# Decode attention beside a Strassen-like feed-forward: summing one step's values directly ahead of the next step's scores

## The reference, cut to what matters

```python
def _sb_block(q_blk, qpos_blk, k, v, k_pos, sb_bias):
    z = jnp.einsum('bqhd,bkhd->bhqk', q_blk, k) * (HEAD_DIM ** -0.5)
    z = z + sb_bias[None, :, None, None]
    mask = k_pos[None, :] < qpos_blk[:, None]
    log1m = jnp.where(mask, jax.nn.log_sigmoid(-z), 0.0)
    suffix = lax.cumsum(log1m, axis=3, reverse=True)
    between = jnp.concatenate([suffix[..., 1:], jnp.zeros_like(suffix[..., :1])], axis=-1)
    a = jnp.where(mask, jnp.exp(jax.nn.log_sigmoid(z) + between), 0.0)
    return jnp.einsum('bhqk,bkhd->bqhd', a, v)
...
past_k = cache_k[l][page_table].reshape(db, past_len, H_SB, HEAD_DIM)
past_v = cache_v[l][page_table].reshape(db, past_len, H_SB, HEAD_DIM)
```

## Time and profile before

| what | value |
|---|---|
| runs before, three | 3337.8, 3342.49, 3342.72 us; median 3342.49 us |
| profiled execution, first to last instruction | 3338.9 us |
| PE matmuls busy | 3206.4 us, 96% |
| PE weight loads busy | 2425.2 us, 73% |
| DVE, ACT, POOL busy | 51%, 34%, 47% |
| moved by DMA | 536.93 MB, mean 161 GB/s |

### The profile page before, as it was taken

One profiled execution on the slowest core, in us unless ns is written; L12 is line 12 of the kernel. 1 busy time (PEld: TensorE's weight loads), 2 busy tenths in 40 slices (PEclk: granted clock), 3 DMA queues, 4 the chain that ended last, 5 costly groups with the idle time before them and its releaser, 6 DMA issues.

```text
span 3338.9 us, 54535 instructions
## 1 busy us (share of the span) xinstructions
PE 3206.4 (96%) x18534; PEld 2425.2 (73%) x18535; DVE 1706.2 (51%) x2588; ACT 1134.6 (34%) x2457; POOL 1578.2 (47%) x1265
## 2 busy tenths in 40 slices
PE   7999999899899899999999999999999999899999
PEld 5777786566566677777777777777777778787777
DVE  4222222499799454545435544454553444665555
ACT  3333333499799333222103312212331220232220
POOL 2322222277576455544445544435554544565553
PEclk9999999999899899999999999999999999999999
DMA  7223311301100567777886767787677655122222
GB/s 275 95 96 118 103 45 37 110 2 52 53 2 14 200 207 254 252 257 249 276 303 209 242 227 234 248 269 258 226 241 234 234 190 172 63 76 76 76 76 83
DMA packets 235494, 536.93 MB, mean 161 GB/s; under 512 B 27599, under 2 KB 57535, under 8 KB 214217
## 3 DMA queue, kind: packets, MB, share of 16 engines
q1 hardware_dynamic: 200072, 354.12, 32.4%
q10 hardware_dynamic: 35137, 179.22, 15.0%
HBM read 498.70 MB, written 34.55 MB: 160 GB/s over the span
## 4 chain that ended last, share of the span: by engine, by line
PE 57%; DVE 6%; issue 2%; DMA 1%; ACT 1%; DVEq 0%; ACTq 0%
PE ff_pB L1694 49%; PE s_pZ L1290 4%; PE s_pO L1304 3%; DVE ff_conv L1986 1%; DVE s_left L1368 1%; DMA ff_w<-in_w_units 1%; DVE ff_act_in L2002 0%; DVE ff_x L1913 0%; ACT ff_conv L1778 0%; PE s_pZ L1296 0%; DVE ff_conv L1988 0%; DVE ff_rs L1995 0%; DVE s_kpage L1979 0%; DVE s_kpage L1976 0%; DVE s_stop L1372 0%
## 5 line engine op out<-in xcount | busy, mean ns | idle before, releaser
L1694 PE MATMUL ff_pB<-ff_act_in,ff_w 128*128 128x256 f32 (+1 forms) x2496 | 617.2, 392 | 22.7 <-ACT ff_act_in L1773 14.6
L1694 PEld LDWEIGHTS ff_pB<-ff_act_in,ff_w 128*128 128x128 f32 x2496 | 475.8, 194 | 133.7 <-issue 45.7
L2042 POOL TENSOR_TENSOR ff_sums<-ff_w 128x512 f32<-128x512 f32 (+1 forms) x152 | 190.4, 1253 | 697.8 <-PE ff_pB L1694 583.1
L1986 DVE SCALAR_TENSOR_TENSOR ff_conv<-ff_raw,k_vecT,ff_conv 128x512 f32<-128x512 f32 x352 | 381.2, 1083 | 91.9 <-ACT ff_raw L1785 85.7
L1913 DVE SCALAR_TENSOR_TENSOR ff_x<-ff_pB,k_mod,ff_x 128x256 f32<-128x256 f32 (+2 forms) x448 | 214.2, 480 | 385.8 <-PE ff_pB L1694 381.9
L1808 ACT ACTIVATE ff_raw<-ff_pB 128x256 f32<-128x256 f32 (+1 forms) x352 | 136.0, 388 | 765.4 <-PE ff_pB L1694 760.0
L1694 PE MATMUL ff_pB<-ff_diff_up,ff_sums 128*128 128x256 f32 (+1 forms) x1600 | 389.0, 385 | 5.6 <-DVE ff_diff_up L1889 5.6
L1184 POOL TENSOR_TENSOR at_stop<-at_stop,at_left 128x512 f32<-128x512 f32 (+3 forms) x320 | 311.5, 998 | 164.5 <-ACT at_stop L1124 160.3
L1962 DVE TENSOR_TENSOR ff_raw<-ff_raw,ff_pB 128x256 f32<-128x256 f32 (+1 forms) x264 | 111.3, 424 | 474.4 <-PE ff_pB L1694 474.4
L1694 PEld LDWEIGHTS ff_pB<-ff_diff_up,ff_sums 128*128 128x128 f32 x1600 | 301.3, 190 | 70.2 <-issue 17.1
L2054 POOL TENSOR_TENSOR ff_raw<-ff_raw,ff_conv 128x512 f32<-128x512 f32 (+1 forms) x88 | 119.3, 1355 | 301.5 <-ACT ff_raw L1791 124.7
(11 more groups left out here) (248 smaller groups left out, 5026.9 us busy)
## 6 DMA issues: line engine op xcount, KB each, us to landing
ff_w<-in_w_units ACTq DMA_DIRECT2D x136, 1024.0 KB, 6.2
s_kpage<-in_cache_k SPq DMA_DIRECT2D x512, 256.0 KB, 4.0
s_vpage<-in_cache_v SPq DMA_DIRECT2D x512, 256.0 KB, 3.1
in_ada<-in_w_ada SPq DMA_DIRECT2D x16, 1024.0 KB, 5.0
ff_w<-in_w_units ACTq DMA_DIRECT2D x16, 768.0 KB, 4.8
in_w<-in_w_in SPq DMA_DIRECT2D x5, 2048.0 KB, 20.1
in_hT<-in_x_cols SPq DMA_DIRECT2D x8, 1024.0 KB, 6.9
wada<-in_w_ada SPq DMA_DIRECT2D x4, 2048.0 KB, 18.2
```

Of the source, the lines that this page charges most:

```text
L1694: last = pe.matmul(into, left[:, kt * P:(kt + 1) * P], right[:, kt, :], start=kt == 0 and p in (1, 2, 5), stop=kt == depth(j) - 1, skip_gr ...
L1986: ins = dve.scalar_tensor_tensor(cv, raw[:, f % 2, half, i:i + CT], tap, cv, ALU.mult, ALU.add)
L2042: pool.tensor_tensor(S3, A11, A21, ALU.subtract).then_inc(sums_ready, 1)
```

## The change

The list of a chunk used to hold four entries per step (SCORE, WEIGH, MOVE, SUM), each placed by itself, evenly. Now it holds three: the SUM of the step before together with SCORE, then WEIGH, then MOVE. SUM of the very last step is an entry of its own. The entries are still spread evenly over the products. No instruction is added or taken away, and no buffer or semaphore is changed.

```diff
-    pieces = [(q, i) for q in steps for i in (SCORE, WEIGH, MOVE, SUM)]
+    pieces = []
+    for q in steps:
+        pieces += [[(q - 1, SUM)] * (q > 0) + [(q, SCORE)], [(q, WEIGH)], [(q, MOVE)]]
+        if q == NSTEP - 1:
+            pieces.append([(q, SUM)])
...
-            plan.append(("sa",) + pieces[placed])
+            plan += [("sa",) + piece for piece in pieces[placed]]
```

## The result

| kernel | median, lowest to highest | ratio to the kernel before, 95% interval |
|---|---|---|
| before | 3340.14 us, 3335.5 to 3342.72 (4 runs) | |
| changed | 3367.65 us, 3357.09 to 3372.01 (4 runs) | 1.0083 [1.0068, 1.0098] |

The change makes the kernel slower by 0.8%, 27.5 us. The forecast of 3333 us and its range up to 3348 are both missed, and the sign is the other one. The profiled execution has a span of 3370.3 us against 3338.9, at the upper end of the runs.

The account below looks back on a forecast made before the run. The prediction took PE to bound the kernel. Its terms, -20.5 - 4 + 2 + 13 = -9.5 us on a 3338.9 us span, gave 3329.4, plus 3.6 to the runs' median: 3333 us, range 3319 to 3348.

Parts of the forecast that it names:

- The visits: PE at SUM and SCORE: 63 joined visits save 0.33 us each if the seam is free, together 20.5 us.
- case D: Rival, between SUM and SCORE: the seam costs what a visit does, giving 3349 us; chance 0.05.
- The distance from SCORE to MOVE: More room from SCORE and WEIGH to MOVE ends PE's waits for `s_stop`: 4 us gained.
- case E: Rival, on DVE and ACT: WEIGH and copies hold up products elsewhere, +5 us, giving 3338; chance 0.12.
- The norms: WEIGH directly ahead of the reciprocal lengthens PE's `ff_act_in` waits in chunks two and three: +2 us; first chunk even.
- The pages: K pages late for SCORE in twelve steps: 14.4 us, less 1.4 of `ff_x` waits, so +13.
- The walk: Step-by-step count of late K pages, steps 2 to 63, arrival minus step length less earlier lateness: 14.4 us.
- my own bound: Upper bound for late K pages: 28.9 us if each page arrives 1 us later.
- case C: Rival, K pages late by more: the page loop paces the first chunk; 3349 us at 1 us more; chance 0.13.
- the signs that I had named: Refuting readings: `s_kpage` row missing or above 25 us, SUM-to-SCORE starts above 1.9, `ff_x` and `ff_raw` waits up 5.
- The sum: All terms on the span of 3338.9 us: -20.5 - 4 + 2 + 13 = -9.5 us.

## Why the prediction was wrong, point by point

**The visits: right.** The price of a visit was read correctly and the seam is free (1.74 us from SUM to SCORE). Of the 20.5 us, 16 were measured in the kernel that has nothing else, with 20.5 inside its interval. My case D, a seam that costs what a visit does, is out: its sign was starts above 1.9 us apart.

**The distance from SCORE to MOVE: the step that failed.** I counted room between WEIGH and MOVE and took 4 us of gain, as if the old waits for `s_stop` were the only thing that WEIGH's place decides. Two things were wrong with that. The room for MOVE moves most of those waits and does not remove them: DVE is as late as before, and the product that needs the next take of `ff_raw` waits instead of MOVE (5.5 us in 8 cases for 4.0 in 8, with MOVE alone moved). And WEIGH is 1.4 to 3.4 us of DVE in a list that DVE must walk in order; its later place sets it ahead of other work, above all of additions to `ff_x` and of the norm. Measured, the new places cost 16 to 18 us, of which MOVE's place has 0.12%, 4 us and within the intervals of nothing, and WEIGH's the rest. I had this as case E with 5 us and a chance of 0.12, priced as "half as much again" of the old waits for `ff_x`, with no reading of what stands around WEIGH at its new places. This is step 11 in the changed kernel, DVE first, then POOL and PE:

```profile
1434.68 1.53 DVE L1990 SCALAR_TENSOR_TENSOR ff_conv<-ff_raw,k_vecT,ff_conv 128x512 f32<-128x512 f32 x2
1436.12 0.15 DVE L1381 COPY s_left<-s_left 128x1 f32<-128x1 f32 x1
1436.31 1.86 DVE L1368 TENSOR_TENSOR_SCAN s_left<-s_go,s_left 128x256 f32<-128x256 f32 x1
1438.20 1.30 DVE L1372 TENSOR_TENSOR s_stop<-s_stop,s_left 128x256 f32<-128x256 f32 x1
1439.43 0.86 DVE L1917 SCALAR_TENSOR_TENSOR ff_x<-ff_pB,k_mod,ff_x 128x256 f32<-128x256 f32 x2
...
1436.35 1.27 POOL L2058 TENSOR_TENSOR ff_raw<-ff_raw,ff_conv 128x512 f32<-128x512 f32 x1 [5.70 <-DVE ff_conv L1990]
1437.70 1.52 POOL L2060 TENSOR_TENSOR ff_hidden<-ff_raw,ff_conv 128x512 f32<-128x512 f32 x1
...
1439.96 3.56 PE L1698 MATMUL ff_pB<-ff_diff_down,ff_sums 128*128 128x256 f32 x8 [2.26 <-DVE ff_x L1917]
1443.35 1.89 PE L1698 MATMUL ff_pB<-ff_hidden,ff_sums 128*128 128x256 f32 x8
```

And the same step on DVE in the kernel before, where no product waits at this place:

```profile
1428.10 0.75 DVE L1368 TENSOR_TENSOR_SCAN s_left<-s_go,s_left 128x256 f32<-128x256 f32 x1
1428.89 0.42 DVE L1372 TENSOR_TENSOR s_stop<-s_stop,s_left 128x256 f32<-128x256 f32 x1
1429.23 0.48 DVE L1913 SCALAR_TENSOR_TENSOR ff_x<-ff_pB,k_mod,ff_x 128x256 f32<-128x256 f32 x1
1429.62 1.53 DVE L1986 SCALAR_TENSOR_TENSOR ff_conv<-ff_raw,k_vecT,ff_conv 128x512 f32<-128x512 f32 x2
```

At its old place WEIGH stood ahead of the last two taps and was done in 1.3 us. At the new one it stands behind them and directly ahead of the additions to `ff_x`, and takes 3.3 us. PE waits 2.26 us for an addition, and then runs at the lower clock: granted 0.61 on the mean of 1440 to 1444 us, with 3.39 us from this product's start to the next one's and not 1.73.

**The norms: right in the second and third chunk, wrong in the first.** The wait for `ff_act_in` rose from 11.2 to 12.6 us in sum. In the first chunk I set gain against loss at nothing; MOVE's wait there was 3.05 us, with a slower clock behind it.

**The pages: the right mechanism, mis-sized.** Twelve late steps were forecast and twelve came, steps 3 and 55 among them, though not all the same ones: step 21, my worst case, was not late. That the number agrees is in part luck. The walk gave 14.4 us and I took 13; the waits were 21.7. By my own bound a mean lateness of half a microsecond more does that, but I have not found where it comes from: the median landing was 3.9 us, not longer than the 4.2 of before. SP's idle time under SUM, which I had expected to shrink, grew from 426.0 to 457.0 us in 63 waits. What I left out altogether is what comes with such waits: the slower clock behind the long ones, and weights that come late (8.5 us against 1.2; 4.5 when pages are issued fast). The experiments price the late pages with all that at 26 to 28 us, twice my term. So case C, at 0.13, is what happened in size, together with E. Of the signs that I had named, that of E came (waits for `ff_x` and `ff_raw` grew by 11.7 us, with 5 as the border); that of C did not (21.7 us for `s_kpage`, with 25 as the border), because the border left out the clock and the weights.

**The sum.** -16 (visits) + 17 (places) + 27 (pages) = 28 us, and 27.5 were measured; since the terms are differences of the same four kernels, this had to come out. Set against my -9.5 us, the visits gave 4.5 us less, the places cost 19 more than my -4 + 2, and the pages 14 more than my 13.

**Where the price of the places goes.** Between the new and the old places with early pages, PE's listed waits differ by 10 us (44.8 against 34.9). Most of the rest is the clock. Over stretches of 2 us between 1150 and 2790 us, one minus the granted clock, times the length, sums to 20.5 us with the new places and to 12.0 with the old ones, 8.5 more (10.2 in the kernel before, 25.6 in the change). The falls that only the new places have come behind MOVE's wait of 3.36 us in the first norm and behind three waits of 2.0 us for `ff_x`. 10 and 8.5 are near the 18 us by the ratios; each trace is one execution. From the change to its kernel with early pages the same two terms give 26 us of waits and 5 of clock, against 26 by the ratios; the profiled execution of the change was the longest of its four.

**What stays open.** Which of the WEIGHs beyond the first carry the places' price was not tried one by one. Why the weights come late at the ends of chunks was not tried either, nor why the page waits came out at 21.7 us and not at 14.4.

The version to keep is the seam with WEIGH and MOVE at their old places and page numbers read early: 3322.19 us, 0.5% under the kernel before. WEIGH a sixth of a step behind SCORE is as good within the intervals.

## What to carry to other kernels

Where two pieces of one tile shape can stand side by side, the saving is the price of a visit, and it can be read ahead from the starts of the products around one. But moving a piece in a list that several engines walk moves three things at once: the transfers that wait for it, the work behind it on the other engines, and PE. Each has to be priced at the new place, from what stands next to it there, and not from the waits of the old place. When a buffer is single, the room of its transfer is the time from the last read to the next, so putting two reads side by side can take that room away; making the issue faster, here by reading numbers ahead of the wait, gives it back.

## What the runs showed of the hardware beyond that

Reading a page number and starting its transfer takes SP 1.1 us a page, and 0.5 us with the number read before (16 issues in 17.6 and 8.4 us). Transfers issued faster land later: for the K pages between 1200 and 1680 us the first line is of the changed kernel, and the second, from the same view, of the one with early page numbers:

```profile
DMA to landing us min/median/max: 2.8/3.9/7.9
```

```profile
DMA to landing us min/median/max: 4.4/5.9/9.8
```

The median grows by 2.0 us, while 9 us of issue are saved.

WEIGH has no fixed length. In the rows of step 11 above, its scan and product took 0.75 and 0.42 us in the kernel before, where POOL had nothing under way, and 1.86 and 1.30 us in the changed kernel, beside two instructions of POOL. The Trainium skill, SBUF — State Buffer, section SBUF: two separate sides, says that DVE, when it reads two operands from SBUF, and a GpSimd instruction that reads SBUF need the same pair of ports, and that the one which comes second is blocked until the first has ended; the lengths of these rows agree with it. I had taken 1.3 us for WEIGH everywhere.
